# Scores of a gated linear recurrence: the blocks of the two largest levels copied last instead of first

## The reference, cut to what matters

```python
def step(state, blk):                       # one chunk, one direction
    qc, kc, vc, gc = blk
    cum = jnp.cumsum(gc, axis=2)
    rel = jnp.where(lower, cum[:, :, :, None, :] - cum[:, :, None, :, :], -jnp.inf)
    scores = jnp.einsum('bhtd,bhsd,bhtsd->bhts', qc, kc, jnp.exp(rel))
    o = (jnp.einsum('bhts,bhsv->bhtv', scores, vc)
         + jnp.einsum('bhtd,bhdv->bhtv', qc * jnp.exp(cum), state))
    cum_end = cum[:, :, -1:, :]
    state = (jnp.exp(cum_end)[:, :, 0, :, None] * state
             + jnp.einsum('bhsd,bhsv->bhdv', kc * jnp.exp(cum_end - cum), vc))
    return state, o
```

## Time and profile before

| | |
|---|---|
| median of 3 runs | 2072.22 us |
| the profiled execution's own time | 2068.54 us |
| its span in the profile | 2066.8 us |
| TensorE busy | 1859.6 us, 90% |
| VectorE busy | 1093.6 us, 53% |
| ScalarE busy | 836.9 us, 40% |
| mean granted clock of TensorE | 0.945 |
| chain that ended last | TensorE 65%, issue 14%, VectorE 9%, ScalarE 6% |

### The profile page before, as it was taken

One profiled execution on the slowest core, in us unless ns is written; L12 is line 12 of the kernel. 1 busy time (PEld: TensorE's weight loads), 2 busy tenths in 40 slices (PEclk: granted clock), 3 DMA queues, 4 the chain that ended last, 5 costly groups with the idle time before them and its releaser, 6 DMA issues.

```text
span 2066.8 us, 27737 instructions
## 1 busy us (share of the span) xinstructions
PE 1859.6 (90%) x11307; PEld 1537.1 (74%) x11307; DVE 1093.6 (53%) x1714; ACT 836.9 (40%) x1234; POOL 81.7 (4%) x135
## 2 busy tenths in 40 slices
PE   5899789898999999989969789896999889999888
PEld 2678566676777778867746579875999778988777
DVE  0341377734444463553367457855656555545773
ACT  2322534423333343352444245643333446556441
POOL 0000001201000000010001100001000010000100
PEclk9999998889999999999969889998999999999888
DMA  9444100013555532334300255543666455555541
GB/s 322 169 149 166 52 1 1 1 62 122 163 163 163 163 123 78 104 109 163 123 0 2 88 166 184 184 153 111 189 188 188 161 150 170 173 167 172 118 57 41
DMA packets 211453, 261.35 MB, mean 126 GB/s; under 512 B 4657, under 2 KB 173283, under 8 KB 211199
## 3 DMA queue, kind: packets, MB, share of 16 engines
q1 hardware_dynamic: 207690, 248.28, 36.9%
q0 software_dynamic: 3232, 11.15, 3.0%
q10 hardware_dynamic: 405, 0.15, 0.0%
HBM read 258.43 MB, written 1.12 MB: 126 GB/s over the span
## 4 chain that ended last, share of the span: by engine, by line
PE 65%; issue 14%; DVE 9%; ACT 6%; DMA 5%; POOL 1%; SPq 0%; DVEq 0%; ACTq 0%; POOLq 0%
PE acc L640 17%; PE acc L642 16%; PE acc L641 16%; PE acc L676 2%; PE acc L820 2%; PE acc L1123 1%; PE acc L852 1%; DMA weights<-in_w_ada_dram 1%; ACT weights_high L1265 1%; DVE scratch L1859 1%; DVE weights_low L1686 1%; DMA weights<-in_w_up_dram 1%; PE acc L1053 1%; PE acc L1099 1%; DMA weights<-in_w_down_dram 1%
## 5 line engine op out<-in xcount | busy, mean ns | idle before, releaser
L1686 DVE TENSOR_TENSOR weights_low<-weights,weights_high 128x2048 fp32r<-128x2048 f32 (+1 forms) x184 | 417.1, 2268 | 634.5 <-ACT weights_high L1265 634.3
L1265 ACT ACTIVATE weights_high<-weights 128x2048 fp32r<-128x2048 f32 (+1 forms) x184 | 348.5, 1896 | 667.4 <-DMA weights<-in_w_up_dram 189.8
L640 PE MATMUL acc<-normed_t_high,weights_high 128*128 128x256 f32 (+1 forms) x1824 | 579.6, 318 | 8.7 <-DVE weights_low L1686 5.5
L642 PE MATMUL acc<-normed_t_high,weights_low 128*128 128x256 f32 (+1 forms) x1824 | 565.1, 310 | 0.0
L641 PE MATMUL acc<-normed_t_low,weights_high 128*128 128x256 f32 (+1 forms) x1824 | 563.8, 309 | 0.0
L640 PEld LDWEIGHTS acc<-normed_t_high,weights_high 128*128 128x128 f32 x1824 | 346.6, 190 | 39.3 <-DVE normed_t_low L1725 8.3
L641 PEld LDWEIGHTS acc<-normed_t_low,weights_high 128*128 128x128 f32 x1824 | 344.5, 189 | 24.1 <-issue 4.3
L642 PEld LDWEIGHTS acc<-normed_t_high,weights_low 128*128 128x128 f32 x1824 | 343.9, 189 | 20.9
L640 PE MATMUL acc<-weights_high,normed_t_high 128*128 128x512 f32 (+1 forms) x792 | 313.6, 396 | 28.9 <-DVE normed_t_low L2026 28.8
L641 PE MATMUL acc<-weights_low,normed_t_high 128*128 128x512 f32 (+1 forms) x792 | 310.1, 392 | 0.0
L642 PE MATMUL acc<-weights_high,normed_t_low 128*128 128x512 f32 (+1 forms) x792 | 309.8, 391 | 0.0
(11 more groups left out here) (221 smaller groups left out, 1907.1 us busy)
## 6 DMA issues: line engine op xcount, KB each, us to landing
weights<-in_w_ada_dram SPq DMA_DIRECT2D x48, 1024.0 KB, 5.5
weights<-in_w_up_dram SPq DMA_DIRECT2D x44, 1024.0 KB, 7.3
weights<-in_attn_w_in_dram SPq DMA_DIRECT2D x40, 1024.0 KB, 5.1
weights<-in_conv_w_in_dram SPq DMA_DIRECT2D x32, 1024.0 KB, 5.8
weights<-in_w_in_dram SPq DMA_DIRECT2D x24, 1024.0 KB, 7.0
weights<-in_w_down_dram SPq DMA_DIRECT2D x20, 1024.0 KB, 5.0
weights<-in_w_out_dram SPq DMA_DIRECT2D x8, 1024.0 KB, 5.0
weights<-in_conv_w_out_dram SPq DMA_DIRECT2D x8, 1024.0 KB, 5.0
```

Of the source, the lines that this page charges most:

```text
L640: pe.matmul(o, ah, bh, start=start, stop=False)
L642: return pe.matmul(o, al, bh, start=False, stop=stop)
L1265: act.activation(hi_slot(n)[:, 0:used], slot(n)[:, 0:used], ACT.Copy).then_inc(hi_in.sem, 1)
L1686: dve.tensor_tensor(slot(n, ring_lo)[:, 0:used], slot(n)[:, 0:used], hi_slot(n)[:, 0:used], ALU.subtract).then_inc(lo_in.sem, 1)
```

## The change

TensorE computes the pairs in the order 0, 1, 2, 3. VectorE no longer waits for ScalarE's copies before its first masked copy. ScalarE's copies of pair 3 now wait for the last masked copy (`taken` of pair 2), and `O` waits for ScalarE's copies.

```diff
@@ TensorE, scores(i) and states(i)
-                        for lp in (3, 0, 1, 2):
+                        for lp in range(4):
                             outs = [open_group(("S", li, i, lp, par)) for par in range(2)]
...
-                            pe.wait_ge(*taken_after(("S", li, i, 2, par)))
+                            pe.wait_ge(*taken_after(("S", li, i, 3, par)))
                             if i >= 2:
@@ ScalarE, large_blocks(i)
                     act.wait_ge(full, full_after(keys[1]))
+                    for par in range(2):
+                        act.wait_ge(*taken_after(("S", li, i, 2, par)))
                     for lo, hi in pairs:
@@ VectorE, masked(i)
                     if is_full(li, i):
-                        for par in range(2):
-                            dve.wait_ge(*taken_after(("S", li, i, 3, par)))
                         for lp in range(3):
```

## The result

The changed kernel is slower: a median of 2081.65 us (2076.95 to 2087.35, 6 runs) against 2071.2 us (2064.63 to 2073.61, 6 runs) of the kernel before on the same chip, a ratio of 1.0056 with a 95% interval of 1.0033 to 1.0078. By that ratio it is 11.6 us more (6.8 to 16.2), and the two medians are 10.4 apart; 13.5 were forecast. The profiled spans are 2066.8 and 2077.1 us, the mean granted clocks 0.945 and 0.946.

What follows compares the result with a forecast made beforehand. The recurrence was taken as bound by a chain of hand-overs, no engine full. Layer 0's 10.9 us plus layer 1's 2.6 gave 13.5 on 2072.2: 2085.7 us, own range 2081 to 2089, 8 in 10 within 2079 to 2093.

Steps and rivals of the forecast that it cites:

- 1.73 us for E1 and E2: Next unit's E1 and E2 wait for pair 2's copies instead of pair 1's, one pair later: 1.73 us.
- The gain of the first copy: VectorE starting pair 0 freely wins 0.60 us at unit 3, 0.1 at units 4 and 6, nothing at 1, 2, 5, 7.
- ScalarE's copies covered: ScalarE's copies, now last, cost nothing where `s` follows the scores: E3 needs their bank only 2.0 us after pair 2.
- The terms of layer 0: Units 1, 2, 5 together 5.2 us, unit 3 1.2, unit 4 1.6, unit 6 1.7, unit 0 0.1, unit 7 1.1; sum 10.9.
- Unit 7: Layer 0's last unit: `O` waits behind ScalarE's copies, 0.96 + 0.1 after pair 2, costing 1.1 us.
- Layer 1: Unit 4 costs 2.1 us, unit 5 1.4, unit 6 0.2, unit 7 gains 1.1; sum 2.6 us.
- No term for the clock: Sum has nothing for the recurrence's unsteady clock, as the looser window was the fast one; a shift gives 3.4 us either way.
- The signs in the profile: Right: 1.5 to 2 us idle before E0, E1. Wrong: line 820 not idle longer, or stages outside moving over 2 us.
- Rival 2: Longer stalls take three windows from clock 1.00 to 0.83, 8.7 us on top of the sum: 2094.4; chance 0.08.
- Rival 3: Later E1 to E3 hidden behind the attention's own chain; only 3.2 us remain, 2075.4; chance 0.05.
- Rival 4: ScalarE's copies behind pair 2 not covered: 1.1 us added at each of eight units, 2094.5; chance 0.05.
- Rival 1: VectorE's start decides and TensorE finds its banks free: all 8.6 us of waits come back, 2063.6; chance 0.04.

Runs made afterwards that it cites:

- the short pair 2: Second masked copy of pair 2 (level 5) left out: 1.0041 in the changed kernel, 0.9997 in the kernel before, both against the kernel before.
- the order alone: The kernel before with only the order of pairs changed to 0, 1, 2, 3, its waits kept: ratio 1.0224, about 46 us slower.
- the run with the early masked copies: The changed kernel with VectorE's masked copies moved ahead of the attention's combination step: ratio 1.0023 to the kernel before.

## Why the prediction was right

The direction, the mechanism and most of the sizes held: the two stages became 12.1 us longer by the profile (13.5 forecast), and the whole kernel, by the runs, 11.6. The forecast median of 2085.7 lies 4.0 above the measured one: 1.0 of it is the kernel before, which took 2071.2 and not 2072.2 in these runs, and 3.0 is the difference of the medians, 10.4 where the sum has 13.5. By its own steps:

- *What bounds the recurrence:* hand-overs of banks. Shown by the short pair 2, which moves the changed kernel's path and not that of the kernel before.
- *1.73 us for E1 and E2:* measured 1.73 in the unit's path, the mean of five units.
- *The gain of the first copy:* nothing at units 1 and 5 and 0.1 us at unit 2, near enough as forecast. Unit 3 won 0.87 us and not 0.60, unit 6 0.71 and not 0.1: its first copy starts 2.79 us behind the first score, 3.50 before. Unit 6 was mis-sized, because I priced only the idle time visible before the copy; VectorE's combination in front of it came earlier against the scores too.
- *ScalarE's copies covered:* shown by taking them out; not at units 7 and at unit 4 of layer 1, where the sum had priced them.
- *The terms of layer 0:* later end of the fourth exponential, counted from each unit's first score: unit 0 0.22 (forecast 0.1), then 2.77, 1.59, 0.91, 1.59, 1.71, 1.07 for units 1 to 6, those six 9.6 in sum where 9.7 was forecast. That they come out so close is in part luck. Unit 1's extra 1.0, which the last section shows to be the clock, makes up for what units 3 and 6 won beyond the forecast.
- *Unit 7:* from the first score to `O` 8.47 us before and 9.57 after, the forecast 1.1. Yet the stage became 1.1 us shorter. TensorE's same instructions took 24.36 us busy instead of 26.45: the clock gave back 2.1. First the window of before, then of after:

```profile
382.40:421.20 38.80, 26.45 (x164) 20.59 (x163) 25.28 (x58) 17.09 (x54) 11.86 (x20) 0.70 0.00 1
```

```profile
393.80:431.50 37.70, 24.36 (x164) 18.87 (x163) 25.30 (x58) 17.16 (x54) 11.88 (x20) 0.79 0.00 1
```

- *Layer 1:* units 4 and 5 together +3.4 from first score to first score (forecast 3.5), unit 6 +0.4 (0.2), unit 7 -1.0 (-1.1).
- *No term for the clock:* right for the sum, wrong for the parts. The "wrong if" of 2 us outside the recurrence was met by the last stage, -3.5 us, where the change has no instruction and the other kernels here range from 903.0 to 913.1 us. I put it down to where the half-speed stretches fall; no run isolates that. The prediction's reason for leaving the clock out is weaker than it reads: in the earlier trace rows the window at 1.00 has 102 matmuls in 16 us and the one at 0.83 has 124 in 20, much the same rate, so the second is busier in good part because it is slower. Those rows can't say what idle time does to the clock.
- *The signs in the profile:* E1 starts 0.1 us after the third pair, as forecast, but the 1.5 to 2 us of idle time expected in front of E0 and E1 aren't there. TensorE idles earlier, before `s` and kT; line 820 waits 2.1 us in 5 cases against 1.8 in 5, so one "wrong if" was nearly met by the letter. The prediction saw that `s` would wait and didn't say that kT would wait longer: it now inherits a bank of pair 1.
- *Rival 2, the clock falls:* not in the mean of the stage (0.90 before and after), but at one unit. The mechanism that the prediction takes from "TensorE: Matmul & The Clock Gate" stands there under "A second HAM failure mode: psum-queue depth-cycling", in the Trainium skill; the stage's 0.90 doesn't bear it out as a general effect here, and unit 1 fits it. *Rival 3, hidden:* refuted by the stage, 10.4 us longer. *Rival 4, uncovered:* refuted by the run without ScalarE's copies. *Rival 1, the early start wins:* even with the copies moved ahead of the combination it wins nothing over the kernel before, since the later bank takes back 1.73 of 1.85 us a unit.

## What to carry over

When buffers are handed out in turn, the order in which a stage fills its buffers is also the order in which the next stage gets them: before reordering, write down who inherits each one, and when its last reader ends. A wait taken off one engine is worth little more than its idle time (8.6 us in sum here, of which 4.2 stayed), while its price is paid by whoever inherits the buffer released last. And a queue behind the moved work is only free as long as something slower covers it: here repairing the bank alone gave 0.24 of 1.7 us.

## What the runs showed of the hardware

The longer stall in front of the E groups at unit 1 of layer 0 cost twice. In the changed kernel TensorE was busy for 0.72 of the 2 us from 277 to 279, and the clock was 0.52 over the next 2 us, close to the lower of its two levels; the 8 matmuls of the groups took 5.15 us instead of 3.9:

```profile
277.00:279.00 2.00, 0.72 (x5) 0.34 (x5) 1.51 (x3) 0.00 (x0) 0.00 (x0) 1.00 0.00 0
279.00:281.00 2.00, 2.00 (x4) 1.00 (x5) 1.70 (x3) 0.33 (x2) 0.00 (x0) 0.52 0.00 0
```

The runs without ScalarE's copies and with the short pair 2 on the changed kernel show the same at the same unit (5.29 and 5.30 us for 8), and so does the order alone (5.08). The kernel before, its variant without ScalarE's copies, the run with the early masked copies and the one with `s` behind the gates keep 1.00 through these groups. That is rival 2 in small: 1.0 us of it is real at this unit. It isn't a rule of the stall's length alone: at unit 2 of the changed kernel waits of 1.19, 1.11 and 0.36 us left the clock at 1.00, and at unit 7 the kernel with the longer wait had the higher clock.

Together the half-speed stretches move a stage of the recurrence by 2 to 3 us with no change in its hand-overs. In the kernel before, its variant without ScalarE's copies and the one with pair 0 first, `O` of unit 7 starts 8.47 to 8.48 us after the first score; the stage from there takes 38.8, 36.1 and 36.9 us, with TensorE busy for 26.5, 24.5 and 23.6. Over all kernels here the same matmuls take 20.9 to 27.4 us. That is as much as most single edits here are worth. A single profile can't judge such an edit by its stage's length. The unit's path, which at units 2 to 6 repeats within 0.1 us in the kernels before and after, can, but only for the hand-overs inside it: the run with the early masked copies lost its gain behind it.
